# Gate tiles of the attention stage: spread over all ticks to the last, instead of the first 24 and the first 16

## What is computed

```python
# block one, one layer (hybrid_mixer): three kinds of attention, 16 heads, 3 x 1024 gates
q_a, k_a, v_a, f_a, q_b, k_b, v_b, q_c, c_kv, q_i, k_i, w_i, gates = split(h @ w_in)
y_a = forgetting_attention(...)       # 6 heads, "fox"
y_b = stick_breaking_attention(...)   # 5 heads, "sb"
y_c = dsa_attention(...)              # 5 heads, "dsa", keys picked by an index score
g_a, g_b, g_c = split(sigmoid(gates), 3)
merged = g_a * (y_a @ w_up_fox) + g_b * (y_b @ w_up_sb) + g_c * (y_c @ w_up_dsa)
# block two, one layer (hybrid_layer): two kinds, 16 heads, 2 x 1024 gates
y_a = swa_attention(...) @ w_o_swa    # 8 heads, "swa"
y_b = moba_attention(...) @ w_o_moba  # 8 heads, "moba"
mixed = sigmoid(gate_a) * y_a + sigmoid(gate_b) * y_b
```

## Time and profile before

| what | value |
|---|---|
| median of 3 runs | 2142.24 us (2140.62 to 2146.01) |
| profiled execution, its own time | 2141.67 us |
| its span, first to last instruction | 2140.0 us |
| mean granted TensorE clock | 0.959 |
| busy: TensorE, weight loads, VectorE, ScalarE | 95%, 87%, 69%, 46% |

### The profile page before, as it was taken

One profiled execution on the slowest core, in us unless ns is written; L12 is line 12 of the kernel. 1 busy time (PEld: TensorE's weight loads), 2 busy tenths in 40 slices (PEclk: granted clock), 3 DMA queues, 4 the chain that ended last, 5 costly groups with the idle time before them and its releaser, 6 DMA issues.

```text
span 2140.0 us, 35880 instructions
## 1 busy us (share of the span) xinstructions
PE 2023.9 (95%) x13708; PEld 1861.0 (87%) x13708; DVE 1468.2 (69%) x2592; ACT 975.0 (46%) x1464; POOL 36.9 (2%) x72
## 2 busy tenths in 40 slices
PE   7999999889999999999889997998899979898998
PEld 6999998879998999999779997897789968887997
DVE  7776558677767776457687776765766678566665
ACT  5335445543344344454644334455444445544443
POOL 0000000000000000000000000000000000000000
PEclk9999999899999999999899997997899999989999
DMA  8774443147764774443247762531354544223453
GB/s 307 269 263 176 179 157 119 63 189 289 272 243 154 276 283 180 167 152 116 80 175 267 270 221 87 208 111 50 126 189 179 196 155 158 109 79 127 178 191 133
DMA packets 76905, 382.14 MB, mean 179 GB/s; under 512 B 8960, under 2 KB 9088, under 8 KB 55552
## 3 DMA queue, kind: packets, MB, share of 16 engines
q1 hardware_dynamic: 67392, 329.78, 42.1%
q0 software_dynamic: 9408, 50.90, 6.8%
HBM read 379.60 MB, written 1.05 MB: 178 GB/s over the span
## 4 chain that ended last, share of the span: by engine, by line
PE 84%; DVE 10%; ACT 3%; issue 2%; DMA 0%; SPq 0%; DVEq 0%; ACTq 0%
PE psum L541 26%; PE psum L542 25%; PE psum L543 25%; DVE weights_low_a L1298 2%; PE psum L823 1%; PE psum L851 1%; PE psum L634 1%; DVE h_low L1349 1%; PE psum L825 1%; ACT weights_high_a L973 1%; PE psum L742 1%; PE psum L824 1%; PE psum L632 1%; PE psum L798 1%; DVE merge_terms L1766 1%
## 5 line engine op out<-in xcount | busy, mean ns | idle before, releaser
L541 PE MATMUL psum<-h_high,weights_high_a 128*128 128x256 f32 x2480 | 712.6, 287 | 16.1 <-DVE h_low L1345 8.0
L542 PE MATMUL psum<-h_low,weights_high_a 128*128 128x256 f32 x2480 | 705.1, 284 | 0.0
L543 PE MATMUL psum<-h_high,weights_low_a 128*128 128x256 f32 x2480 | 704.5, 284 | 0.0
L1298 DVE TENSOR_TENSOR weights_low_a<-raw_a,weights_high_a 128x2048 fp32r<-128x2048 f32 (+1 forms) x232 | 460.1, 1984 | 111.6 <-ACT weights_high_a L973 108.9
L541 PEld LDWEIGHTS psum<-h_high,weights_high_a 128*128 128x128 f32 x2480 | 478.3, 193 | 30.2 <-issue 12.0
L542 PEld LDWEIGHTS psum<-h_low,weights_high_a 128*128 128x128 f32 x2480 | 479.1, 193 | 7.1 <-issue 1.0
L543 PEld LDWEIGHTS psum<-h_high,weights_low_a 128*128 128x128 f32 x2480 | 478.5, 193 | 0.0
L973 ACT ACTIVATE weights_high_a<-raw_a 128x2048 fp32r<-128x2048 f32 (+1 forms) x232 | 387.0, 1668 | 159.5 <-PE psum L543 155.6
L1298 DVE TENSOR_TENSOR weights_low_b<-raw_b,weights_high_b 128x1024 fp32r<-128x1024 f32 x224 | 273.5, 1221 | 78.5 <-ACT weights_high_b L973 77.5
L973 ACT ACTIVATE weights_high_b<-raw_b 128x1024 fp32r<-128x1024 f32 x224 | 237.6, 1061 | 162.0 <-PE psum L543 162.0
L541 PE MATMUL psum<-weights_high_b,gated_high 128*128 128x512 f32 x608 | 241.1, 396 | 0.0
(11 more groups left out here) (276 smaller groups left out, 2841.3 us busy)
## 6 DMA issues: line engine op xcount, KB each, us to landing
ada_weights<-in_w_ada POOLq DMA_DIRECT2D x64, 768.0 KB, 4.7
raw_a<-in_w_ffn_a_a SPq DMA_DIRECT2D x44, 1024.0 KB, 6.8
raw_a<-in_w_ffn_b_a SPq DMA_DIRECT2D x44, 1024.0 KB, 6.9
raw_a<-in_w_ffn_a SPq DMA_DIRECT2D x64, 512.0 KB, 4.4
raw_b<-in_w_ffn_b SPq DMA_DIRECT2D x64, 512.0 KB, 3.5
raw_a<-in_w_proj_a SPq DMA_DIRECT2D x28, 1024.0 KB, 5.7
raw_a<-in_w_gate_a SPq DMA_DIRECT2D x26, 1024.0 KB, 4.8
raw_b<-in_w_ffn_a_b SPq DMA_DIRECT2D x44, 512.0 KB, 3.5
```

The lines of the kernel that those rows point to most:

```text
L541: pe.matmul(out, l_hi, r_hi, start=start, stop=False, skip_group_check=True)
L542: pe.matmul(out, l_hi, r_lo, start=False, stop=False, skip_group_check=True)
L543: return pe.matmul(out, l_lo, r_hi, start=False, stop=stop, skip_group_check=True)
L1298: dve.tensor_tensor(wlo[kind][:, p, 0:width], raw[kind][:, p, 0:width], whi[kind][:, p, 0:width].bitcast(F32), ALU.subtract).then_inc(lo_r ...
```

## The change

The tick of a gate tile now comes from a table for each block, and the number of the tile, not of the tick, sets which part is split next. Block one has no gate tile in ticks 7, 12, 17, 20 and 23, and has one in each of 24 to 28. Block two has them in ticks 0 to 6 and then in every other tick up to 24. Nothing is added or taken away. The core of the diff:

```diff
+GATE_TICKS = {1: [t for t in range(29) if t not in (7, 12, 17, 20, 23)],
+              2: [0, 1, 2, 3, 4, 5, 6, 8, 10, 12, 14, 16, 18, 20, 22, 24]}
+
+
+def gate_of(blk, tick):
+
+    return GATE_TICKS[blk].index(tick) if tick in GATE_TICKS[blk] else None
...
-                for tick in range(max(len(items) + 3, gates)):
-                    if tick < gates:
-                        gate_tile(l, blk, walk, tick)
+                for tick in range(len(items) + 3):
+                    g = gate_of(blk, tick)
+                    if g is not None:
+                        gate_tile(l, blk, walk, g)
...
-                act.activation((g1 if blk == 1 else g2)[:, tick, :], ps[:, tick % 2, 0:SEQ],
+                act.activation((g1 if blk == 1 else g2)[:, g, :], ps[:, g % 2, 0:SEQ],
...
-                    if tick < gates and tick % 3 == 0:
-                        split_high(l, blk, 1, n0 + tick // 3 + 1)
+                    if g is not None and g % 3 == 0:
+                        split_high(l, blk, 1, n0 + g // 3 + 1)
                     if tick in TOKEN_WORK_ACT[blk]:
                         TOKEN_WORK_ACT[blk][tick]()
-                    if tick < gates:
-                        gate_tile(blk, walk, tick, gates)
-                        if tick % 3 == 1 or (blk == 2 and tick == 15):
-                            split_high(l, blk, 0, n0 + tick // 3 + 2)
+                    if g is not None:
+                        gate_tile(blk, walk, g)
+                        if g % 3 == 1 or (blk == 2 and g == 15):
+                            split_high(l, blk, 0, n0 + g // 3 + 2)
...
-                for tick in range(max(len(items) + 4, gates + 1)):
+                for tick in range(len(items) + 4):
+                    g, before = gate_of(blk, tick), gate_of(blk, tick - 1)
...
-                    if tick < gates and tick % 3 == 0:
-                        split_low(l, blk, 1, n0 + tick // 3 + 1)
-                    before = tick - 1
-                    if 0 <= before < gates and (before % 3 == 1 or (blk == 2 and before == gates - 1)):
+                    if g is not None and g % 3 == 0:
+                        split_low(l, blk, 1, n0 + g // 3 + 1)
+                    if before is not None and (before % 3 == 1 or (blk == 2 and before == gates - 1)):
                         split_low(l, blk, 0, n0 + before // 3 + 2)
```

More of the change, by code:

```diff
@@ L1162, in item_copy, with gate_tile @@
                                ACT.Copy).then_inc(now().pt_copied, 1)
-            def gate_tile(blk, walk, tick, gates):
-                mark = walk.mark[tick]
+            def gate_tile(blk, walk, g):
+                mark = walk.mark[g]
                 act.wait_ge({"a": now().used[0], "b": now().used[1], "g": now().group_done}[mark[0]], mark[1])
-                act.activation((g1 if blk == 1 else g2)[:, tick, :], ps[:, tick % 2, 0:SEQ],
+                act.activation((g1 if blk == 1 else g2)[:, g, :], ps[:, g % 2, 0:SEQ],
                                ACT.Copy).then_inc(now().gate_copied, 1)
```

## The result

| | before | change |
|---|---|---|
| median, 16 runs each | 2144.19 us (2135.28 to 2146.56) | 2149.83 us (2147.69 to 2151.4) |
| ratio of the times, 95% interval | 1 | 1.0032 (1.0024 to 1.004) |
| profiled execution, its own time | 2141.67 us | 2149.11 us |
| its span | 2140.0 us | 2147.3 us |
| mean granted clock | 0.959 | 0.966 |

The forecast was 2145.4 us, range 2135 to 2156. The time is in the range, 4.4 us above the forecast; 2.0 of the 4.4 lie in the kernel before, whose median of 3 runs was 2142.24 and whose median of 16 is 2144.19. The difference was forecast at +3.2 us, and is +5.6 by the medians and +6.9 by the ratio. The interval of the ratio lies above 1, and around the 0.3% that the prediction gives as what a measurement of this kernel can tell from no change. The clock, as a mean, rose, and the kernel is still slower.

A forecast was written before the change was run, and what follows sets the result against it. TensorE, 84% of the chain, was taken as the bound, so moved tiles count only through its waits or clock. Block one +1.4 us a layer, block two +1.1 and -0.7, gave +3.2 together: 2145.4 us, range 2135 to 2156.

The forecast's parts named there:

- The emptied ticks become waits: Attention stages: TensorE waits where gate tiles were taken, such as 2.5 us in block one's tick 12.
- the circle: Block one's stick-breaking ticks: VectorE and ScalarE set the pace, 5.5 us a tick, so two tiles less shorten nothing by themselves.
- The tails: Block one, ticks 24 to 28: 20.1 us with no wait, before 12.44; tick 24 starts at 98.0 us, before 105.3.
- Waits should sum to some 13 us in each stage: Attention stages of both blocks: TensorE's waits total some 13 us each; under 6 in the thinned ticks would refute the prediction.
- The carrying: Both stages: three engine queues followed tick by tick at full clock; block two about 85.5 us, against 88.1 and 89.9.
- The clock term: Half clock behind new waits of TensorE: 1.0 us a layer in block one, 2.7 in block two.
- The sum: Four attention stages: block one +1.4 us a layer, block two +1.1 and -0.7, together +3.2 us.
- The sums of work: TensorE's work in the attention stages at full clock: 105 us in block one, 72.4 in block two.
- the second rival: Attention stages: every wait is covered and only work is left, 58 us less, 2084 us; chance 0.03.
- The third, half clock behind most waits: The 14 thinned places: next tile takes 4.5 us, not 3.0, in most; +17 us, 2159; chance 0.24.
- The first, that the clock holds: Attention stages: TensorE stays at clock 1.00; -6 us, to -12, in the middle 2133; chance 0.14.
- The fourth, ScalarE in block one's tail: Block one's tail: ScalarE becomes the bound, up to 4.3 us a tick; +2 us a layer, 2149; chance 0.09.

The follow-up runs named there:

- The reordered copy: The change, but in tick 11 of block one ScalarE copies turn 3 ahead of the split of part a; 2141.18 us, ratio 0.9997 to the kernel before.
- the returned tiles of ticks 17 and 20: The change, but block one has gate tiles again in ticks 17 and 20 and none in 27 and 28; 2141.36 us, ratio 0.9994 to the kernel before.
- spare matmuls in the waits: The change plus matmuls nobody reads where TensorE waits, 44 a layer of block one and 72 of block two; 2137.54 us, ratio 0.9976 to the kernel before.
- Lending from other ticks: The kernel before, but block one has no gate tiles in ticks 3, 7, 11, 27, 28, and block two skips ten other ticks; 2107.32 us, ratio 0.9839.

## Why the prediction was right, and where it was off

**The emptied ticks become waits: right.** Tick 12 of block one: 2.5 us predicted, 2.36 measured in both layers, for the copy of turn 3 behind the split. Tick 17: 1.4 predicted, 1.29 measured. Tick 20: 1.3 and 3.1 predicted, 0.67 and 2.87 measured. Tick 23: 1.4 predicted, 0.43 and 0.81 measured in the two layers.

| block two, tick | 7 | 9 | 11 and 13 | 15 | 21 | 23 | 25 |
|---|---|---|---|---|---|---|---|
| predicted | 2.3 | 2.2 and 0.6 | 0.5 and 0.3 | 1.9 | 1.9 | 1.0 | 2.3 |
| measured | 2.44 | 2.21 and 0.39 | one of 0.19 | 1.62 | 1.76 | 0.96 | 2.23 |

The reordered copy takes one of the causes away, and the wait goes with it; the returned tiles of ticks 17 and 20 show that two tiles fit into the circle at a price of 0.3 us. The waits of block two, tick 7 apart, were read from the queues and not tested one by one. Of tick 7 of block two the text named moba's scaling alone; the split ahead of it is the other half.

**The tails: right.** Block one's last five ticks take 407.97 - 387.75 = 20.2 us at clock 1.00, and 20.1 were predicted. They start 100.6 and 99.1 us after the stage's start, where 98.0 were predicted; with spare matmuls in the waits it is 97.5. One step on the way was wrong in size: a split that leaves the stick-breaking ticks was to shorten them by 2.3 us, and they took 21.2 us in place of 22.1. (The 7.3 us that tick 24 was to come earlier are also not four fifths of the 15.2 us of the five tiles, as the prediction has it, but about half.)

**"Waits should sum to some 13 us in each stage": right for block two, 11.8; wrong for block one, 7.8 and 9.4.** The carrying took every operation at full clock. In the stick-breaking ticks the circle of VectorE and ScalarE (scan, add, absolute value; exp and ln) sets the pace, and a tile at half clock fills a part of the wait. Windows of the change over these four ticks, in the first and the second layer:

```profile
357.38:378.54 21.16, 17.39 (x108) 15.97 (x108) 17.24 (x35) 11.48 (x20) 0.00 (x0) 0.76 0.22 75
1015.10:1036.30 21.20, 16.24 (x111) 14.13 (x111) 17.28 (x34) 12.26 (x21) 0.00 (x0) 0.84 0.23 77
```

In the first layer the clock is 0.76, the wait of tick 18 is gone and that of tick 19 is 0.23. In the second the clock is 0.84 and they are 0.58 and 0.83. The ticks take 21.2 us in both, and also with the spare matmuls at clock 1.00. There half clock is free.

**The clock term, "I take 1.0 and 2.7 us": the term that was mis-sized.** For the four layers it made 7.4 us; the spare matmuls brought back 11.8, 4.4 more. The allowance was half of 1.5 us for each wait, two waits in block one and five in block two. That rule gives 1.5 and 3.75 a layer, 10.5 in all, and the text took 1.0 and 2.7 without a reason: most of the miss is there. The rule also counted waits, and not what lay behind them. Block two lost 3.9 and 3.3 us a layer, close to the rule's 3.75. Block one lost 3.1 and 1.6, behind tick 12 alone: there the fox pair, outside the circle, lost 2.6 and 1.6 by itself, and the waits of ticks 17 and 20 had nothing to lose. The price of a wait is the wait, and the work at half clock behind it where nothing else sets the pace.

**The sum.** Block one was to be +1.4 a layer, and is +2.7 and +1.6. Block two was to be +1.1 and -0.7, and is +2.2 and +0.3. All four are above, together by 3.5 us (6.7 against 3.2). Of the four stage lengths only block one's 124.8 lies where the prediction said it would; its 126.3 is above 125.5, and block two's two of 95.9 are above 95. Where the 3.5 come from can be told. Without the clock term the forecast for the four stages is 436.2 + 3.2 - 7.4 = 432.0 us, and with the clock at 1.00 by the spare matmuls they took 431.1. So the queues, with the 1 us a layer of block two that was added because the carrying had fallen short before, were right within 0.9 in their sum, and the miss is the clock term: 4.4 - 0.9 = 3.5.

The sums of work were too small, 105 and 72.4 us where stages at clock 1.00 show 106.8 and 74.8. That the queues came out right is therefore in part luck. In block two the work was 2.4 us a layer too small, the waits 1.2 too large (13.0 against 11.8), and 1 was added: 86.4 to the last values, and 86.6 with the spare matmuls. In block one the work was 1.8 too small, and what stood beside it some 2 too large. The best case of the second rival, work alone, is too good by the same 8 us.

**The rivals.** The third, half clock behind most waits, is what goes on, but not at its price: it gave +17 us, and +6.9 came by the ratio. The first, that the clock holds, fell: the clock was 0.85 and 0.93 in the thinned parts. With spare matmuls in the waits the clock does hold, and then the time is 2137.5, near what it gave (-6). The fourth, ScalarE in block one's tail, fell: TensorE is busy for 20.48 of 20.48 us there. The second, that every wait is covered (2084), isn't reached by this table. Lending from other ticks brought 36 us of its 58, and with the work as measured some 50 were there to be had.

The Trainium skill ("Perfetto Trace Analysis", Optimization Strategy) says that interleaving regimes with different bounds may improve performance. The runs here agree with one table and not with another: the same kind of move gave +0.3% and -1.6%.

## What to carry to other kernels

Lend cover for a sparse tail from ticks where its absence opens no wait: look, for each tick, at what the bound engine does next, at what that waits for, and at what stands ahead of the producer in its queue; then lend from a tick where the producer is done. Work that hangs on the number of the moved piece (here the splits) moves too, and decides as much as the piece itself. Price a new wait by its length and by the half clock behind it (2.36 us cost 2.6 and 1.6 more here), and where a wait can't be avoided, see whether matmuls that nobody reads pay for themselves.

## What the runs showed that I had not expected

Matmuls whose results are never read made the kernel faster: 158 of them took 9.4 us off the time of before (2143.01 to 2133.6), and 232 some 12 off the change. No run has both the lent cover and spare matmuls. A wait of 2.36 us was followed by a fox pair of 5.62 us in one layer and 4.62 in the other, and one of 0.56 us by the same pair in 3.03. A turning that leaves TensorE idle is also paid for behind itself, in the up matmuls. And the mean clock is no measure of gain: it rose from 0.959 to 0.966 while the kernel grew slower by 0.3%.
